# Second gated layer: four gate blocks that multiply the tokens alone go first, and the hand-over makes the token tiles before the context's

## The reference, cut to what matters

```python
h = rms_norm(x, norm_w[layer]) * (1.0 + scale) + shift
hc = rms_norm(xc, norm_w[layer]) * (1.0 + scale_c) + shift_c
if last:
    proj_kv_c = hc @ w_in[layer][:, KV_START:KV_END]
...
u, v_sgu, za, q, k, v, zb = jnp.split(h @ w_in[layer], SPLIT_POINTS, axis=-1)
...
sgu = chunk_sgu(u, v_sgu, w_sgu[layer], b_sgu[layer], v_norm_w[layer])
y = jnp.concatenate([sgu * silu(za), merge_heads(attn) * silu(zb)], axis=-1) @ w_out[layer]
x = x + gate * y
```

## Time and profile before

| | |
|---|---|
| median of three executions | 3429.25 us (3427.72 to 3437.78) |
| profiled execution | 3425.83 us, span 3423.7 us |
| TensorE busy | 3276.4 us, 96% of the span |
| VectorE, ScalarE, GpSimd busy | 66%, 54%, 14% |
| mean granted TensorE clock | 0.986 of 2.4 GHz |
| the hand-over between the two gated layers | from 846.8 to 887.2 us |

### The profile page before, as it was taken

One profiled execution on the slowest core, in us unless ns is written; L12 is line 12 of the kernel. 1 busy time (PEld: TensorE's weight loads), 2 busy tenths in 40 slices (PEclk: granted clock), 3 DMA queues, 4 the chain that ended last, 5 costly groups with the idle time before them and its releaser, 6 DMA issues.

```text
span 3423.7 us, 54987 instructions
## 1 busy us (share of the span) xinstructions
PE 3276.4 (96%) x22635; PEld 2907.8 (85%) x22635; DVE 2273.8 (66%) x3091; ACT 1842.0 (54%) x2904; POOL 475.9 (14%) x739
## 2 busy tenths in 40 slices
PE   7999999999999999999999999999999999899997
PEld 3688788787789999999998878888879888899996
DVE  3688889823654556666766576676676555799856
ACT  2344444322566646676775355555546564677644
POOL 0010111111000000000000014877020000322001
PEclk9999999999999999999999999999999999999999
DMA  9755566722234555555554546665545435455454
GB/s 354 279 179 173 185 216 219 278 99 93 95 115 149 178 179 186 185 176 194 179 179 163 181 151 202 217 214 198 171 155 173 136 124 166 154 165 169 161 179 142
DMA packets 175322, 608.45 MB, mean 178 GB/s; under 512 B 21888, under 2 KB 21920, under 8 KB 173408
## 3 DMA queue, kind: packets, MB, share of 16 engines
q1 hardware_dynamic: 145440, 495.54, 43.0%
q0 software_dynamic: 28624, 105.72, 9.0%
q10 hardware_dynamic: 1008, 3.67, 0.3%
HBM read 596.27 MB, written 8.57 MB: 177 GB/s over the span
## 4 chain that ended last, share of the span: by engine, by line
PE 73%; DVE 9%; ACT 8%; DMA 7%; issue 3%; SPq 0%; ACTq 0%; DVEq 0%
PE psum_all L587 21%; PE psum_all L583 16%; PE psum_all L585 15%; PE psum_all L580 10%; DMA raw<-in_stream 5%; ACT w_hi L510 2%; DVE w_lo L517 2%; DMA mod_early<-in_stream 1%; DVE xT L876 1%; ACT ssd_seg L2286 1%; PE psum_all L1558 1%; PE psum_all L1528 1%; PE psum_all L748 1%; PE psum_all L3145 1%; DVE ln_d L1098 1%
## 5 line engine op out<-in xcount | busy, mean ns | idle before, releaser
L587 PE MATMUL psum_all<-act_parts,w_lo 128*128 128x256 f32 (+1 forms) x6704 | 2007.2, 299 | 0.0
L517 DVE TENSOR_TENSOR w_lo<-raw,w_hi 128x1024 fp32r<-128x1024 f32 x866 | 1064.7, 1245 | 804.4 <-ACT w_hi L510 803.0
L583 PE MATMUL psum_all<-act_parts,w_hi 128*128 128x256 f32 (+1 forms) x4464 | 1408.2, 315 | 39.6 <-DVE act_parts L975 16.9
L585 PE MATMUL psum_all<-act_parts,w_hi 128*128 128x256 f32 (+1 forms) x4464 | 1378.2, 309 | 0.0
L510 ACT ACTIVATE w_hi<-raw 128x1024 fp32r<-128x1024 f32 x866 | 906.5, 1056 | 787.0 <-DMA raw<-in_stream 785.8
L587 PEld LDWEIGHTS psum_all<-act_parts,w_lo 128*128 128x128 f32 x6704 | 1282.2, 191 | 41.6
L583 PEld LDWEIGHTS psum_all<-act_parts,w_hi 128*128 128x128 f32 x4464 | 857.5, 192 | 110.2 <-issue 42.4
L585 PEld LDWEIGHTS psum_all<-act_parts,w_hi 128*128 128x128 f32 x4464 | 858.2, 192 | 43.0 <-issue 3.6
L580 PE MATMUL psum_all<-act_parts,w_hi 128*128 128x512 f32 x2240 | 799.8, 401 | 25.9 <-DVE w_lo L517 13.8
L580 PEld LDWEIGHTS psum_all<-act_parts,w_hi 128*128 128x128 f32 x2240 | 422.0, 188 | 135.0 <-issue 22.0
L876 DVE SCALAR_TENSOR_TENSOR xT<-mod_late,small,xT 128x1024 f32<-128x1024 f32 x210 | 256.7, 1279 | 8.2 <-DMA mod_late<-in_stream 5.8
(11 more groups left out here) (498 smaller groups left out, 3407.7 us busy)
## 6 DMA issues: line engine op xcount, KB each, us to landing
raw<-in_stream SPq DMA_DIRECT2D x858, 512.0 KB, 3.3
mod_late<-in_stream POOLq DMA_DIRECT2D x128, 512.0 KB, 4.6
mod_early<-in_stream SPq DMA_DIRECT2D x128, 256.0 KB, 6.1
ssd_seg<-acs_rows POOLq DMA_DIRECT2D x8, 1536.0 KB, 6.6
s_matrices<-s5p_made POOLq DMA_DIRECT2D x16, 384.0 KB, 3.4
raw<-in_stream SPq DMA_DIRECT2D x16, 256.0 KB, 4.8
s_made<-s_matrices POOLq DMA_DIRECT2D x16, 256.0 KB, 3.0
xT<-in_x SPq DMA_DIRECT2D x1, 2048.0 KB, 10.2
```

The lines of the kernel that those rows point to most:

```text
L517: dve.tensor_tensor(w_lo[:, n % RING, :], raw[:, n % RING, :], w_hi[:, n % RING, :].bitcast(F32), ALU.subtract).then_inc(lo_ready, 1)
L583: pe.matmul(sums, w_hi[:, n % RING, cols], block.rhs(kk, HIGH, block.width), start=(kk == 0), stop=False)
L585: pe.matmul(sums, w_hi[:, n % RING, cols], block.rhs(kk, LOW, block.width), start=False, stop=False)
L587: last = pe.matmul(sums, w_lo[:, n % RING, cols], block.rhs(kk, HIGH, block.width), start=False, stop=(kk == block.kt - 1))
```

## The change

The second layer has an order of its own, `LAST_ORDER`: za0 to za3, then what was there, without them; za4 to za7 stay at the end. The stream of the weights follows that order. Four blocks instead of two run in halves, and they are za0 to za3, in PSUM banks 6, 7, 2, 3; k0, k1, v0, v1 run whole behind them. The 16 pairs of the hand-over are all eight of the tokens and then all eight of the context. VectorE has 6 of the 32 `whole` steps instead of 9. Units 2 to 8 instead of 2 to 4 are split between the pairs, at places given by `units_behind` (units 2, ..., 8 behind pairs 5, 7, 8, 10, 11, 13, 14). TensorE waits for token pairs in za0 and for context pairs in k0. Four more buffers of 1 KB hold silu(za0) to silu(za3) until u is ready; their gating now comes in the slots of vg and u.

```diff
-LEAD = dict(gate_in1=2, fox_in=3, mla_in=3, s5_in=2, s5_glu=4)
+LEAD = dict(gate_in1=4, fox_in=3, mla_in=3, s5_in=2, s5_glu=4)
...
+LAST_ORDER = [("za", i) for i in range(LEAD["gate_in1"])] \
+    + [block for block in LAYER_ORDER if block[0] != "za" or block[1] >= LEAD["gate_in1"]]
+LAYER_ORDERS = [LAYER_ORDER, LAST_ORDER]
...
-                    before.begin_scalar(act, lambda i: split_hi(act, n0 + AHEAD + (i >= 3) + (i >= 5)))
+                    before.begin_scalar(act, lambda i: split_hi(act, n0 + i if before.by_units
+                                                                else n0 + AHEAD + (i >= 3) + (i >= 5)))
...
-                    before.begin_vector(dve, lambda i: split_lo(dve, n0 + AHEAD + (i >= 5) + (i >= 7)))
+                    before.begin_vector(dve, lambda i: split_lo(dve, n0 + i if before.by_units
+                                                                else n0 + AHEAD + (i >= 5) + (i >= 7)))
...
                 self.affine([((ctxT if v else self.tmp)[:, k:k + 2, :],
                               [(mod_col(1, KT + i, v), mod_col(1, i, v),
-                                "dve" if i % 2 and (v or k == 0) else "act")
+                                "dve" if i % 2 and k % (8 if v else 4) == 0 else "act")
                                for i in (k, k + 1)], pair_of(act_hi, v * KT, k), pair_of(act_lo, v * KT, k))
-                             for k in range(0, KT, 2) for v in range(2)])
+                             for v in range(2) for k in range(0, KT, 2)])
+                self.units_behind = {5: 3, 7: 4, 8: 5, 10: 6, 11: 7, 13: 8, 14: 9}
...
-                    split(i // 2)
+                    split(self.units_behind.get(i, 0))
...
-                k, v = i // 2 * 2, i % 2
+                v, k = i // (KT // 2), i % (KT // 2) * 2
...
-                        split((i - 2) // 2)
-
-            def wait_tile(self, pe, k):
-                pe.wait_ge(self.low.sem, self.low.at(k // 2 * 2 + 2))
+                        split(self.units_behind.get(i - 2, 0))
+
+            def waits(self, layer):
+                return {LAST_ORDER[0]: self.wait_token_tile, ("k", 0): self.wait_context_tile}
+
+            def wait_token_tile(self, pe, k):
+                pe.wait_ge(self.low.sem, self.low.at(k // 2 + 1))
+
+            def wait_context_tile(self, pe, k):
+                pe.wait_ge(self.low.sem, self.low.at(KT // 2 + k // 2 + 1))
...
-                self.s_gate, self.s_split = by_slot("za", 1), {min(at["za", i] + 2, n): [] for i in range(8)}
-                for i in range(8):
-                    self.s_split[min(at["za", i] + 2, n)].append(i)
+                self.s_gate, self.s_split = {max(at["za", i] + 1, at["vg", i] + 5): i for i in range(8)}, {}
+                for slot, i in self.s_gate.items():
+                    self.s_split.setdefault(min(slot + 1, n), []).append(i)
...
-            za = [at_work(f"za{layer}_{s}", [P, width], 62 + 2 * s) for s in range(2)]
+            za_pair = [at_work(f"za{layer}_{s}", [P, width], 62 + 2 * s) for s in range(2)]
+            za_kept = [at_work(f"za{layer}_kept_{i}", [P, width], 40 + i) for i in range(lead if last else 0)]
+            za = za_kept + [za_pair[i % 2] for i in range(len(za_kept), SGU_GROUPS)]
...
-            for i in range(0 if last else QUARTERED):
-                blocks[i].place = i
+            for block, bank in zip(blocks, (6, 7, 2, 3) if last else range(QUARTERED)):
+                block.place = bank
```

More of the change, by code:

```diff
@@ L281, in sequence @@
             units = []
-            for kind, i in LAYER_ORDER:
+            for kind, i in LAYER_ORDERS[int(name[-1])]:
                 section, block = LAYER_PLACE[kind]
@@ L908, in build @@
         class Hand:
-            first_slot, counts, opened = 0, (), 0
+            first_slot, counts, opened, by_units = 0, (), 0, False
+            def waits(self, layer):
+                return {LAYER_ORDERS[layer][0]: self.wait_tile}
             def attach(self, first_slot, blocks):
@@ L1278, in build @@
         class SecondInput(Affine):
+            by_units = True
             def __init__(self, sum_bank, root_bank):
@@ L1413, in build, with __init__ @@
         class LayerSlots:
-            def __init__(self, lead, lag, turn):
-                at = self.at = {block: g + lead for g, block in enumerate(LAYER_ORDER)}
-                n = self.n_in = len(LAYER_ORDER) + lead
+            def __init__(self, blocks, lead, lag, turn):
+                at = self.at = {block: g + lead for g, block in enumerate(blocks)}
+                n = self.n_in = len(blocks) + lead
                 def by_slot(first, behind):
@@ L1444, in layer_flow @@
             lead = LEAD["gate_in1"] if last else 3 * QUARTERED
-            at_slot = LayerSlots(lead, lag, 2 if last else 3)
+            at_slot = LayerSlots(LAYER_ORDERS[layer], lead, lag, 2 if last else 3)
             at, n_in = at_slot.at, at_slot.n_in
@@ L1790, in s_gate @@
                 dve.wait_ge(order["vector"].sem, order["vector"].n)
-                dve.tensor_tensor(u[:, i, :], u[:, i, :], za[i % 2][:, :], ALU.mult).then_inc(s_gated.sem, 1)
+                dve.tensor_tensor(u[:, i, :], u[:, i, :], za[i][:, :], ALU.mult).then_inc(s_gated.sem, 1)
             def head_split_low(dve, h):
@@ L1874, in take @@
                 def take(act, ps):
-                    if i >= 2:
+                    if i >= len(za_kept) + 2:
                         act.wait_ge(s_gated.sem, s_gated.at(i - 1))
-                    return act.activation(za[i % 2][:, :], ps, ACT.Silu)
+                    return act.activation(za[i][:, :], ps, ACT.Silu)
                 return take
@@ L1921, in layer_flow @@
             blocks = [Block(KT, TT if name in "kv" else width, both, takes[name](i),
-                            wait=None if (name, i) != LAYER_ORDER[0] else before.wait_tile,
-                            shape=in_halves if last and name in "kv" else None) for name, i in LAYER_ORDER]
-            for i in range(0 if last else QUARTERED):
-                blocks[i].place = i
+                            wait=before.waits(layer).get((name, i)),
+                            shape=in_halves if last and name in "kv" else None) for name, i in LAYER_ORDERS[layer]]
+            for block, bank in zip(blocks, (6, 7, 2, 3) if last else range(QUARTERED)):
+                block.place = bank
             blocks = halves_first(blocks, lead) if last else quarters_first(blocks, QUARTERED)
```

## The result

The changed kernel took 3437.2 us (median, 3430.18 to 3445.0) against 3431.43 us (3427.29 to 3437.78) for the kernel before on the same chip: ratio 1.0015, 95% interval [1.0008, 1.0022]. I had forecast 3426.9 us, a small gain within 0.3%. It is within 0.3%, but on the other side, and above my range. The same changed kernel, run again later, had a ratio of 0.9995 [0.9984, 1.0006]. So whole times settle little here; stretches of the profile settle more.

What follows compares the result with a forecast made beforehand. VectorE's list of splits was taken to bound the hand-over. An earlier start (1.3 us) and fewer losses (1.1) made 2.4 us, taken from the median 3429.25 to forecast 3426.9 us, range 3418.5 to 3435.

Steps and rivals of the forecast that it cites:

- The opening: Hand-over into the second layer, from first product through za0 to za3, k0 and k1: 2.4 us shorter.
- earlier start: First product of the second layer needs pair 0 alone instead of pairs 0 and 1: 1.3 us earlier.
- fewer losses: TensorE's waits and slow clock in the hand-over: 7.2 us lost against 8.3 before, 1.1 us gained.
- The layout of the engines: ScalarE's and VectorE's new hand-over order laid end to end with instruction prices: za3 ends at 886.1 us.
- Rival B: Za halves: waits at units do not come, TensorE is dense from pair 3; gain 5.7 us, 3420.1 us; chance 0.10.
- Rival C: Za halves: clock stays at 1.2 GHz through all eight, kernel 9 us slower, 3435 us; chance 0.06.
- Rival D: Hand-over: ScalarE stands at a load or take, delaying later pairs; loss of 2 to 3 us, 3428.5; chance 0.08.
- Edits at nothing: Loads, takes of za0 to za3 and moved gating: between -0.3 and +0.5 us together, taken as 0.
- rival E: Q and zb slots: the 2.4 us gained are given back in waits for probabilities and ropes; 3425.8 us; chance 0.06.

Runs made afterwards that it cites:

- before_slot16: The kernel before, with TensorE's code aligned to slot 16 of its 256-instruction packets ahead of the second layer's first product, no work changed; ratio 1.0008.
- place 177: The kernel before, with TensorE's code aligned to place 177 of a 256-instruction block at the end of the hand-over's transposes; ratio 1.0032 in both runs.
- place 16: The changed kernel with TensorE's code aligned to slot 16 of its 256-instruction packets behind the spreading matmuls; ratio 0.9986, then 1.0001.
- early units: The changed kernel with units 2 and 3 split ahead of the pairs; ratio 0.9999, and 0.9992 with place 16 added.

## Why the prediction was wrong

- **The opening was right.** Forecast 2.4 us: 1.3 earlier start, 1.1 fewer losses. Measured 3.3. Of this 0.9 is the clock: the spreading matmuls took 1.16 us in after and 2.07 in before. Among profiles with the fast ones, before_slot16 has its first product 9.43 us after the first sum and k1's end at 39.48, the changed kernel 8.23 and 60.11 - 23.04 = 37.07: 1.2 us earlier start, 2.4 in all.
- **The layout of the engines was right**: VectorE's waits for ScalarE 3.5 us in 7 places (forecast 3.3 in 7), TensorE's waits for units 3.0 (2.5 to 3.5), for pairs 4.2 (4.5), VectorE busy 87% of 33 us (over 85%), za3's end 885.1 on the time scale of before (886.1), no wait in k0. The four waits for units came where the layout had them (0.80, 0.73, 0.65 and 0.84 us for units 2, 3, 5 and 7).
- **Rival B** fell: the waits for units came. **Rival C** fell: the clock was back at 863.99 (the next matmuls are 0.12 us apart), as the earlier trace rows spoke for; five waits of 0.53 to 0.84 us between bursts did not bring it down: from 863.99 to 891.00 the granted clock was 1.00, with TensorE busy 23.46 of 27.01 us. So for this pattern the measurement decides against the rule of the Trainium skill that the prediction cites (TensorE: Matmul & The Clock Gate, "A second HAM failure mode: psum-queue depth-cycling"). The page's own case is another one, matmuls of 512 columns in bf16. **Rival D** fell in its place (no load of weights in the opening of after took over 3.6 us), but its mechanism, ScalarE standing at a late landing, is what happened 100 us later. The 4.8 us that the prediction calls the slowest raw loads of the page are the median of 16 loads of 256 KB, not an upper end: in the q and zb slots of before alone, three loads of 512 KB took 4.21, 4.24 and 4.93 us.
- **The failed step is "Edits at nothing"**, and with it rival E. The step priced loads, takes and gating around the hand-over between -0.3 and +0.5 us and took the q and zb slots as untouched, because their instructions are. They took 161.3 us instead of 155.8. I had E give back 2.4 us with a chance of 0.06; it gave back 5.5, more than the gain, through a cause that I had not named. What I should have counted is instructions: 384 moved past the heads are one and a half code packets, and in the heads a late weight load is on the path (the chain: load, high part, two table loads, probabilities, rope). The move by half a period could not have been called good or bad from the page alone, but the heads of before have loads of 4.21 and 4.93 us with a code load 0.69 and 2.78 us behind the issue, 1.0 to 1.7 over the rest. On the path in several heads that makes a term of 0 to +6 us by my estimate, and a wider upper end.
- **The size of the miss in whole time.** Result and forecast are 10.3 us apart. The median of before was 2.2 us higher than the one I started from. The heads add 5.5, the stretches behind them 0.5, and the opening gained 0.9 more than forecast. Some 3 us are left that these profiles do not place. They may be scatter: the changed kernel's later median was 3430.81, and the ratios of the changed order with its own place or, by the count, the same one are 1.0015, 0.9995 and 1.0008, mean 1.0006, 2.1 us, near the +2.6 us of the stretches. But 1.0015 has an interval from 1.0008 to 1.0022, so this part stays open.

That the place of TensorE's code makes the 5.5 us is shown, by moving it in both kernels: the changed order comes down to 155.8 us, the untouched order goes up to 164.6. That it does so through late landings rests on the same load with and without a code load behind it (4.29 and 3.26 us), the chain from it, and the 43 loads against 461; one profile stands behind most places. The path by which a 16 KB packet delays 512 KB of weights is only argued: in this stretch a packet takes 0.9 to 1.7 us, about what the load loses. Open is why place 177 costs the kernel before 0.3% twice: the q and zb slots explain 0.7 and 3.8 us of 11. The later layers took 2132.9 and 2134.2 us in its profiles, against 2126.0 and 2127.9 in the two of before, but before_slot16 had 2138.0 there at a ratio of 1.0008, so one profile can't place the rest. Both ratios of place 177 rest on five executions each. No version beat the kernel before in a way that came back: place 16 had 0.9986 and then 1.0001, with early units 0.9992 [0.9982, 1.0001].

## What to carry to other kernels

When blocks are moved past others in a long unrolled program, count the instructions that move, not only their time: the code is loaded too, by DMA, and where its period is near a stage's period it can hit the same load in several turns running (three of eight heads here, up to seven at other places). Look in each repeated stage for the one load that nothing hides and ask what else is on the DMA queues in the first microsecond behind its issue. And where a stage of unchanged code becomes longer, compare landings before looking for a reason in the change's logic.

## What the runs showed of the hardware

- TensorE's code comes by DMA, 16,384 bytes per packet and 180 packets in the program. The Trainium skill says so too (Runtime: NRT & Kernel Launch, "Instruction fetch mechanics": refills in blocks of 256 instructions by a DMA queue of the sequencer's own, their cost mostly hidden). The trace agrees on the block, one per 251 recorded instructions, and on the engine's own cost: in the changed kernel one wait of TensorE, of 0.4 us, has no releaser that the profile shows. But the refill is not free for others: 3.91 us in the mean instead of 3.24 for a 512 KB load issued 0 to 1.25 us ahead of it, 4.73 at most.
- The same kernel with its code shifted by some places, with the same matmuls and weight loads, differs by up to 10 us in the q and zb stretch (154.6 to 164.6 in the kernel before), and by 0.3% in whole time (1.0032 twice at place 177).
- Short waits of TensorE that went away came together with more time at the low clock: 0.83 granted instead of 0.94 over the eight halves, and the same end.
